# First query projection from features that are scaled by the gain alone, with the token's norm factor applied to its results

## The chip, the cores and the metric

The kernel runs on one core of one Trainium2 chip. The metric is the device time of one execution in microseconds, as the median of several runs. Five engines work side by side: TensorE (PE, with its weight loads as PEld), VectorE (DVE), ScalarE (ACT), GpSimd (POOL) and SyncE (SP), which here issues nearly all DMAs. Each takes its instructions in order, and semaphores tie them together.

## What is computed

The program runs three blocks one after the other over 256 tokens of 1024 features. Only the start of the first block matters here:

```python
def rmsnorm(x, g):
    xf = x.astype(jnp.float32)
    y = xf * lax.rsqrt(jnp.mean(xf * xf, axis=-1, keepdims=True) + EPS)
    return (y * g.astype(jnp.float32)).astype(x.dtype)

h = rmsnorm(x, attn_norm_g)
m = rmsnorm(mem, mem_norm_g)
proj = h @ w_in
da_q, da_k, da_v, wa_q, wa_k, wa_v, xa_q, gates = jnp.split(proj, offsets, axis=-1)
```

Here `da_q` is the first query projection, 1024 columns of `w_in`. After the attention block come a mixture of 16 experts (each with some 25 MB of weights), a second block of two attention layers, and a third block of feed-forward, gating and recurrent layers.

## The kernel before

Activations lie feature-major: 8 blocks of 128 features on the partitions, each with 256 tokens (so a tile of 128x256 is one block, called f or k below). Every dense product is made of three passes in a reduced format: a float32 matrix is split into a high part (rounded, type fp32r) and a low part (the rest), and `t_three` issues high times high (L578), high times low (L579) and low times high (L580).

Weights come from memory in loads of 1 MB, which are numbered: loads 0 to 3 are the four chunks of the first query projection (`daq`), loads 4 to 7 those of the first key projection (`dak`), and so on. They go into four staging slots in turn. ScalarE makes the high part in two halves (`a_hi`, L540, 128x1024 each), then VectorE the low part in two halves (`v_lo`, L551), and both write one of two pairs of buffers, so that load i+2 can be split only as TensorE has read load i, half by half. A chunk of a projection is 48 matrix products of 128x256: half 0 of its weights (blocks k 0 to 3) and then half 1 (k 4 to 7), each for two output tiles. The result of a chunk fills one PSUM bank of 128x512.

The start of the program goes so. ScalarE squares x (L882, four instructions). TensorE sums the squares over the features with a matrix of 1/1024 (L873, `t_rms`), then runs eight products without use on the table `ones` (`t_idle`, L623). ScalarE takes the root (L900, `a_sd`), VectorE the reciprocal (L905, `v_rstd`) into the tile RSTD. Then VectorE makes the normed x block by block (L912: x times gain times RSTD), ScalarE rounds it to the high part (L895, `a_normed`), VectorE subtracts to get the low part (L918), and TensorE starts chunk 0 of `daq` as soon as block 0 is there. All of the nine projections of x read this one pair H.

ScalarE copies each bank of `daq` out with the factor 0.125 (L831). The norm of the second input `mem` follows the same pattern during `dak` and overwrites RSTD. The order on each engine is written out by hand (`t_mix`, `a_mix`, `v_mix`). Projections are generators whose steps are called in turn: one step splits load c+1, the next takes the result of chunk c out. SyncE issues the loads in order and waits, before each, until the two splits of the slot's earlier load have been made.

Of the kernel before, what the change touches and what calls it, by code (L numbers as in the profile page):

```python
# [8 lines left out]
ALU = mybir.AluOpType  # L9
ACT = mybir.ActivationFunctionType  # L10
AX = mybir.AxisListType
P = 128
T = 256
# [148 lines left out]
class Ring:  # L162
# [3 lines left out]
    def next(self):  # L166
        self.i += 1
        return self.ids[(self.i - 1) % len(self.ids)]
# [22 lines left out]
def run(g):  # L191
    for _ in g:
        pass


def F(ap, n=8):
    return ap.rearrange("p (f t) -> p f t", f=n)


def f_(ap):  # L200
    return ap.bitcast(F32)
# [6 lines left out]
def tm(ap):  # L208
    return ap.rearrange("p (t n) -> p t n", t=2)


def both(pair, fn):
    return fn(pair[0]), fn(pair[1])


def it(bank):
    return bank.rearrange("p (i t) -> p i t", t=T)
# [11 lines left out]
class Program:  # L229
# [58 lines left out]
    def B(self, i, n=1):  # L288
        return self.U_(12 + 2 * i, 2 * n)
# [894 lines left out]
    def mix_places(self):  # L1184
        B, R = self.B, self.R
        self.x = B(0)
        self.H = both(self.XP, F)
        self.mp = both(self.pr(6, 7), F)
        self.daq, self.dak, self.dav, self.waq, self.mk, self.mv, self.xaq = B(3), B(4), B(5), B(6), B(9), B(8), B(1)
        self.wak, self.wav = F(B(7)[:, 0:512], 2), tm(B(7)[:, 1024:1536])  # L1190
        self.odt, self.merged = B(2), B(5)
        self.op, self.xp2, self.mgp = self.pr(3, 4), self.pr(6, 2), self.pr(8, 9)
        self.NLAM, self.SUBG = self.LV[:, 5:6], self.LV[:, 6:7]

    def t_mix(self, e):
        DB, KB, OB = Ring(0, 1), Ring(2, 3, 4, 5, 6, 7, 0, 1), Ring(6, 7)
        H, mp, act = self.H, self.mp, self.act
        for w in self.Tw.new(self.first_all):
            e.wait_ge(*w)
        self.t_rms(e, "n1", self.B(9), KB)  # L1200
        self.t_idle(e, 7, 8)
        daq = self.t_proj(e, "daq", 4, H, self.halves("n1"), DB, self.by_act("daq"))
        run(daq)
        dak = self.t_proj(e, "dak", 4, H, self.halves("n1"), KB, self.by_act("dak"))
        next(dak)
        for w in self.Tw.new(self.rest_all):
# [83 lines left out]
    def a_mix(self, e):  # L1290
        act = self.act
        for j in range(4):
            self.a_square(e, "n1", self.x, self.B(9), j, [self.first_all])
        self.a_hi(e, 0, 0)
        self.a_sqrt_table(e)
        self.a_hi(e, 0, 1)
        self.a_sd(e, "n1", 1e-6)
        self.a_next = 1
        self.a_upto(e, 1)
        self.a_normed(e, "n1", self.B(8), self.XP)  # L1300
        daq, dak = self.a_proj(e, "daq", 4, self.a_copy(F(self.daq), 0.125)), self.a_proj(e, "dak", 4, self.a_copy(F(self.dak)))
        for step in range(7):
            next(daq)
        for w in self.Aw.new(self.rest_all, self.dve.val("lam_sums")):
            e.wait_ge(*w)
        e.activation(self.LV[:, 2:4], self.LV[:, 0:2], ACT.Exp).then_inc(*act.inc("lam_exp"))
# [4 lines left out]
        for c in range(4):  # L1311
            next(dak)
            if c == 0:
                self.a_sd(e, "mem", 1e-6)
            next(dak)
            self.a_normed(e, "mem", self.B(8), self.pr(6, 7), range(2 * c, 2 * c + 2))
# [81 lines left out]
    def v_mix(self, e):  # L1398
        dve, LV, LAM = self.dve, self.LV, self.LAM
        for eps, column in self.EPS.items():  # L1400
            e.memset(column, eps).then_inc(*dve.inc(*(["eps"] if eps == 64e-5 else [])))
        for w in self.Vw.new(self.first_all):
            e.wait_ge(*w)
        self.v_upto(e, 0)
        self.v_rstd(e, "n1")
        run(self.v_normed(e, "n1", self.x, self.B(8), lambda f: ("attn_norm_g", f), self.XP))
        daq, dak = self.v_proj(e, "daq", 4), self.v_proj(e, "dak", 4)
        for step in range(5):
            next(daq)
        for w in self.Vw.new(self.rest_all):  # L1410
# [116 lines left out]
        def gained(e, name, c):  # L1527
            residual(e, name, c)
            for f in (2 * c, 2 * c + 1):
                for w in self.Vw.new(dve.val(("out", name, c))):  # L1530
                    e.wait_ge(*w)
                e.tensor_scalar(F(self.h2)[:, f, :], F(self.x)[:, f, :], self.V("ffn_norm_g", f), None, ALU.mult).then_inc(*dve.inc(("ffn", "o", f)))
# [1852 lines left out]
```

## Time and profile before

| | us |
|---|---|
| median of 3 runs | 2803.73 |
| lowest and highest | 2801.77, 2806.78 |
| the profiled execution | 2804.14 |
| its span in the trace | 2802.1 |

| engine | busy, us | share of the span |
|---|---|---|
| PE (matrix products) | 2345.7 | 84% |
| PEld (weight loads) | 1675.2 | 60% |
| DVE | 1227.8 | 44% |
| ACT | 932.8 | 33% |
| POOL | 61.2 | 2% |

All times of the trace are from the start of the span. The profile says busy time per engine; the two stretches to look at are the first 60 us, in which the change lies, and 420 to 1344 us, in which the experts' weights stream in and the DMA engines are full. Where a group of instructions is given with its count, its time runs from the start of the first to the end of the last, and instructions of one engine overlap a little: two of one kind that follow each other start closer together than one lasts.

### The profile page before, as it was taken

The page shows a single profiled execution, that of the slowest core. Times are in us where ns is not written, and L with a number is a line of the kernel's source. Part 1 is how long each engine was busy: PE and PEld are TensorE (multiplying, and loading weights), DVE is VectorE, ACT ScalarE, POOL GpSimd, SP SyncE. Part 2 cuts the span into 40 slices and gives each one's busy share as a digit, 9 for nine tenths or more (in the row PEclk, how much of TensorE's full clock was granted, in tenths as well). Part 3 has the DMA queues.
Part 4 walks back from the last instruction along what each step waited for, and adds up shares of the span by engine and source line. Part 5 has one row for each costly group of instructions (what it writes and reads, how often), then busy time and mean ns, then how long its engine had stood idle before and what let it go on. Part 6 is the DMA issues. An engine that isn't in the chain of part 4 may idle for free.

```text
span 2802.1 us, 37705 instructions
## 1 busy us (share of the span) xinstructions
PE 2345.7 (84%) x16482; PEld 1675.2 (60%) x16482; DVE 1227.8 (44%) x1751; ACT 932.8 (33%) x1524; POOL 61.2 (2%) x36
## 2 busy tenths in 40 slices
PE   8999998656665665566889899999999999977998
PEld 8897784111211121111668778888787888876787
DVE  5567562000100010000476755576656547744654
ACT  5556541000000000000455544354444444632442
POOL 0000010000000000000000000000000000041000
PEclk9999999878888788877989999999999999999999
DMA  7543469999999999999624265575555653412552
GB/s 237 171 157 117 139 209 418 428 428 428 427 428 428 427 428 427 428 428 428 236 76 148 96 198 191 178 241 195 180 181 185 195 206 106 155 34 77 185 191 91
DMA packets 248645, 695.46 MB, mean 248 GB/s; under 512 B 11648, under 2 KB 191104, under 8 KB 222112
## 3 DMA queue, kind: packets, MB, share of 16 engines
q1 hardware_dynamic: 246176, 679.16, 63.7%
q0 software_dynamic: 2016, 13.67, 1.4%
q8 instruction: 130, 2.13, 0.3%
q14 instruction: 35, 0.29, 0.0%
q10 hardware_dynamic: 288, 0.22, 0.0%
HBM read 691.96 MB, written 1.05 MB: 247 GB/s over the span
## 4 chain that ended last, share of the span: by engine, by line
PE 57%; DMA 29%; DVE 8%; ACT 3%; issue 2%; SPq 1%; POOL 0%; DVEq 0%; ACTq 0%
PE ps L578 15%; PE ps L580 15%; PE ps L579 15%; DMA af<-in_w_exp_up 15%; DMA af<-in_w_exp_gate 7%; DMA af<-in_w_exp_down 6%; PE ps L1654 2%; DVE ar L551 2%; PE ps L2594 1%; SPq L509 1%; PE ps L873 1%; PE ps L1684 1%; ACT af L1053 1%; PE ps L2189 1%; DVE af L1089 1%
## 5 line engine op out<-in xcount | busy, mean ns | idle before, releaser
L578 PE MATMUL ps<-ar 128*128 128x512 f32 (+2 forms) x2648 | 928.0, 350 | 27.8 <-DVE ar L551 7.4
L580 PE MATMUL ps<-ar 128*128 128x512 f32 (+2 forms) x2648 | 909.6, 344 | 0.0
L579 PE MATMUL ps<-ar 128*128 128x512 f32 (+2 forms) x2648 | 909.6, 343 | 0.0
L551 DVE TENSOR_TENSOR ar<-af,ar 128x1024 fp32r<-128x1024 f32 x516 | 604.3, 1221 | 290.3 <-ACT ar L540 290.2
L578 PEld LDWEIGHTS ps<-ar 128*128 128x128 f32 x2648 | 504.2, 190 | 104.9 <-issue 11.6
L540 ACT ACTIVATE ar<-af 128x1024 fp32r<-128x1024 f32 x516 | 511.3, 1047 | 164.5 <-PE ps L580 149.1
L580 PEld LDWEIGHTS ps<-ar 128*128 128x128 f32 x2648 | 504.5, 191 | 59.2
L579 PEld LDWEIGHTS ps<-ar 128*128 128x128 f32 x2648 | 505.0, 191 | 56.2 <-issue 0.5
L1654 PE MATMUL ps<-af 128*32 128x512 f32 x2048 | 325.5, 769 | 233.3 <-DMA af<-in_w_exp_up 126.8
L1654 PEld LDWEIGHTS ps<-af 128*32 128x32 f32 x2048 | 63.6, 126 | 480.1 <-DMA af<-in_w_exp_up 199.5
L1823 DVE TENSOR_TENSOR af<-af,ps 128x512 f32<-128x512 f32 x16 | 11.0, 687 | 541.0 <-ACT af L1730 541.0
L1684 PE MATMUL ps<-af 128*32 128x512 f32 x1024 | 168.9, 790 | 93.8 <-DMA af<-in_w_exp_down 82.4
L1730 ACT ACTIVATE af<-ps 128x512 f32<-128x512 f32 x16 | 9.6, 597 | 593.6 <-PE ps L1654 593.6
L1541 DVE TENSOR_TENSOR af<-ps,af 128x512 f32<-128x512 f32 x76 | 48.5, 684 | 299.6 <-PE ps L1696 270.3
L1684 PEld LDWEIGHTS ps<-af 128*32 128x32 f32 x1024 | 35.2, 129 | 210.2 <-DMA af<-in_w_exp_down 140.3
L1737 ACT ACTIVATE af<-ps 128x512 f32<-128x512 f32 x16 | 9.6, 597 | 269.1 <-PE ps L1684 269.1
L2249 DVE TENSOR_TENSOR af<-af,ps 128x256 f32<-128x256 f32 x66 | 27.8, 421 | 125.0 <-ACT af L2220 124.9
L2220 ACT ACTIVATE af<-ps 128x256 f32<-128x256 f32 x66 | 25.3, 384 | 135.7 <-PE ps L580 135.7
L1053 ACT ACTIVATE af<-af,sm 128x256 f32<-128x256 f32 (+1 forms) x136 | 64.0, 474 | 17.1 <-DVE sm L1136 10.2
L2594 PE MATMUL ps<-af 64*64 64x64 f32 x2304 | 44.3, 229 | 20.8 <-issue 16.7
L2594 PEld LDWEIGHTS ps<-af 64*64 64x64 f32 x2304 | 41.2, 141 | 24.5 <-issue 20.0
L2211 ACT ACTIVATE ar<-ps 128x512 fp32r<-128x512 f32 x44 | 26.3, 598 | 81.6 <-PE ps L2189 81.6
(313 smaller groups left out, 1634.8 us busy)
## 6 DMA issues: line engine op xcount, KB each, us to landing
af<-in_w_exp_gate SPq DMA_DIRECT2D x64, 2048.0 KB, 41.2
af<-in_w_exp_up SPq DMA_DIRECT2D x64, 2048.0 KB, 40.8
af<-in_w_exp_down SPq DMA_DIRECT2D x63, 2048.0 KB, 41.5
af<-in_ffn_w_in SPq DMA_DIRECT2D x88, 1024.0 KB, 5.8
af<-in_ffn_w_out SPq DMA_DIRECT2D x44, 1024.0 KB, 5.1
af<-in_w_in SPq DMA_DIRECT2D x34, 1024.0 KB, 5.2
af<-in_sgu_w_in SPq DMA_DIRECT2D x16, 1024.0 KB, 7.0
af<-in_w_out SPq DMA_DIRECT2D x12, 1024.0 KB, 5.3
```

What stands on the lines that cost most here:

```text
L509: e.dma_start(view(base), src).then_inc(*(self.row_in[r] if q == self.tail else self.landed[load.slot]).one())
L540: e.activation(self.WH[load.pair][:, c], self.base(i)[:, c], ACT.Copy).then_inc(*self.act.inc(("hi", i, h)))
L551: e.tensor_tensor(self.WL[load.pair][:, c], self.base(i)[:, c], f_(self.WH[load.pair][:, c]), ALU.subtract).then_inc(*self.dve.inc(("lo", ...
L578: e.matmul(o, lh, rh, start=start, stop=False, skip_group_check=True)
L579: e.matmul(o, lh, rl, start=False, stop=False, skip_group_check=True)
L580: return e.matmul(o, ll, rh, start=False, stop=stop, skip_group_check=True)
L873: m = e.matmul(self.bank(name)[:, 0:T], self.C("ones"), F(tmp)[:, f, :], start=first and n == 0, stop=last and n == len(fs) - 1, skip_grou ...
L1053: e.activation(d, d, ACT.Exp, bias=st[:, g:g + 1], accum_out=st[:, 4 + g:5 + g]).then_inc(*self.act.inc((name, "e", i, g)))
L1541: e.tensor_tensor(d, it(self.bank((name, c))), d, ALU.add).then_inc(*self.dve.inc(("out", name, c)))
L1654: t = e.matmul(ps[32 * j:32 * j + 32, bb, :], XE[:, k, c:c + 32], k_(self.base(q), 2)[:, r, 512 * j:512 * j + 512], start=k == 0, stop=k == 7)
L1684: t = e.matmul(ps[o:o + 32, b, :], self.AT_[x % 2][:, r * P + 32 * j:r * P + 32 * j + 32], k_(self.base(q), 4)[:, r, 512 * c:512 * c + 512 ...
L2594: t = e.matmul(self.ps[64 * r:64 * r + 64, banks[n], 64 * c:64 * c + 64], left(tt, h, i, cp), right(tt, h, i, cp), start=True, stop=True)
```

## The change

A new pair of tiles, `xg`, holds x times the gain (`attn_norm_g`), high and low part, without the token's factor. It lies in room that is free until the norm of `mem` needs part of it. ScalarE makes the high parts (`gained`, a Copy with a scale per partition) and VectorE the low parts (`gained_lo`), in turn with the two halves of load 0. `daq` multiplies `xg`, and needs neither root nor reciprocal. Each chunk's result is then taken out by VectorE instead of ScalarE, in `q_out`: times 0.125 and times RSTD. The eight products without use are gone. The pair H is still made, for the other projections, but later: VectorE makes its parts behind `q_out` of chunks 0 to 2, and ScalarE behind the splits of loads 2, 3 and 4. One wait is added: ScalarE takes the root for `mem`, which overwrites RSTD, only when VectorE has taken out chunk 3.

```diff
+        self.xg = both(self.pr(5, 6), F)
...
-        self.t_idle(e, 7, 8)
-        daq = self.t_proj(e, "daq", 4, H, self.halves("n1"), DB, self.by_act("daq"))
-        run(daq)
+        run(self.t_proj(e, "daq", 4, self.xg, self.halves("xg"), DB, self.by_dve("daq")))
...
+        gained = lambda j: self.a_gained_hi(e, "xg", self.x, self.xg[0], lambda f: self.V("attn_norm_g", f), j, [])
+        gained(0)
         self.a_hi(e, 0, 0)
+        gained(1)
+        self.a_hi(e, 0, 1)
+        gained(2)
+        gained(3)
         self.a_sqrt_table(e)
-        self.a_hi(e, 0, 1)
         self.a_sd(e, "n1", 1e-6)
         self.a_next = 1
         self.a_upto(e, 1)
-        self.a_normed(e, "n1", self.B(8), self.XP)
-        daq, dak = self.a_proj(e, "daq", 4, self.a_copy(F(self.daq), 0.125)), self.a_proj(e, "dak", 4, self.a_copy(F(self.dak)))
+        daq, dak = self.a_proj(e, "daq", 4), self.a_proj(e, "dak", 4, self.a_copy(F(self.dak)))
         for step in range(7):
             next(daq)
+            if step in (2, 4, 6):
+                self.a_normed(e, "n1", self.B(8), self.XP, {2: (0, 1, 2), 4: (3, 4, 5), 6: (6, 7)}[step])
...
             if c == 0:
+                for w in self.Aw.new(self.dve.val(("out", "daq", 3))):
+                    e.wait_ge(*w)
                 self.a_sd(e, "mem", 1e-6)
...
-        self.v_upto(e, 0)
+        def gained_lo(j):
+            for f in (2 * j, 2 * j + 1):
+                for w in self.Vw.new(self.act.val(("xg", "h", f))):
+                    e.wait_ge(*w)
+                e.scalar_tensor_tensor(out=self.xg[1][:, f, :], in0=F(self.x)[:, f, :], scalar=self.V("attn_norm_g", f), in1=f_(self.xg[0][:, f, :]),
+                                       op0=ALU.mult, op1=ALU.subtract).then_inc(*dve.inc(("xg", "l", f)))
+        gained_lo(0)
+        self.v_lo(e, 0, 0)
+        gained_lo(1)
+        self.v_lo(e, 0, 1)
+        self.v_next = 1
+        gained_lo(2)
+        gained_lo(3)
         self.v_rstd(e, "n1")
-        run(self.v_normed(e, "n1", self.x, self.B(8), lambda f: ("attn_norm_g", f), self.XP))
-        daq, dak = self.v_proj(e, "daq", 4), self.v_proj(e, "dak", 4)
+        n1 = self.v_normed(e, "n1", self.x, self.B(8), lambda f: ("attn_norm_g", f), self.XP)
+
+        def q_out(e, name, c):
+            for w in self.Vw.new(self.pe.val(("ps", name, c)), dve.val(("n1", "rstd"))):
+                e.wait_ge(*w)
+            e.scalar_tensor_tensor(out=F(self.daq)[:, 2 * c:2 * c + 2, :], in0=it(self.bank((name, c))), scalar=0.125,
+                                   in1=self.RSTD.unsqueeze(1).broadcast_to((P, 2, T)), op0=ALU.mult, op1=ALU.mult).then_inc(*dve.inc(("out", name, c)))
+            for step in range(4 if c < 2 else 2 if c == 2 else 0):
+                next(n1, None)
+        daq, dak = self.v_proj(e, "daq", 4, q_out), self.v_proj(e, "dak", 4)
```

The first instructions of VectorE before, from the two halves of load 0 (`sm` holds RSTD, `ar` the split pairs, `vec` the gains):

```order
L551 TENSOR_TENSOR ar<-af,ar 128x1024 x2
L905 RECIPROCAL sm<-sm 128x256
L912 SCALAR_TENSOR_TENSOR af<-af,vec,sm 128x256 x3
L918 TENSOR_TENSOR ar<-af,ar 128x256
L912 SCALAR_TENSOR_TENSOR af<-af,vec,sm 128x256
```

The same place on VectorE now, up to the first halves of load 2 (L1415 is `gained_lo`, L1430 is `q_out`):

```order
L1415 SCALAR_TENSOR_TENSOR ar<-af,vec,ar 128x256 x2
L551 TENSOR_TENSOR ar<-af,ar 128x1024
L1415 SCALAR_TENSOR_TENSOR ar<-af,vec,ar 128x256 x2
L551 TENSOR_TENSOR ar<-af,ar 128x1024
L1415 SCALAR_TENSOR_TENSOR ar<-af,vec,ar 128x256 x4
L905 RECIPROCAL sm<-sm 128x256
L551 TENSOR_TENSOR ar<-af,ar 128x1024 x2
L1430 SCALAR_TENSOR_TENSOR af<-ps,sm 128x512
L912 SCALAR_TENSOR_TENSOR af<-af,vec,sm 128x256 x3
L918 TENSOR_TENSOR ar<-af,ar 128x256
L912 SCALAR_TENSOR_TENSOR af<-af,vec,sm 128x256
L918 TENSOR_TENSOR ar<-af,ar 128x256
```

The halves of load 1 stand ahead of the normed blocks now, and directly behind the reciprocal.

ScalarE before, from the squares to the first result taken out:

```order
L882 ACTIVATE af<-af 128x512 x4
L540 ACTIVATE ar<-af 128x1024
L753 ACT_TABLE_LOAD
L753 ACTIVATE sm<-sm 128x1
L540 ACTIVATE ar<-af 128x1024
L900 ACTIVATE sm<-ps,sm 128x256
L540 ACTIVATE ar<-af 128x1024 x2
L895 ACTIVATE ar<-af 128x256 x8
L831 ACTIVATE af<-ps 128x512
```

ScalarE now, over the same part (L1876 is `gained`):

```order
L882 ACTIVATE af<-af 128x512 x4
L1876 ACTIVATE ar<-af,vec 128x256 x2
L540 ACTIVATE ar<-af 128x1024
L1876 ACTIVATE ar<-af,vec 128x256 x2
L540 ACTIVATE ar<-af 128x1024
L1876 ACTIVATE ar<-af,vec 128x256 x4
L753 ACT_TABLE_LOAD
L753 ACTIVATE sm<-sm 128x1
L900 ACTIVATE sm<-ps,sm 128x256
L540 ACTIVATE ar<-af 128x1024 x4
L895 ACTIVATE ar<-af 128x256 x3
L540 ACTIVATE ar<-af 128x1024 x2
```

The root (L900) and the halves of load 1 (the first two of the L540 x4) have moved behind eight gained blocks and the table load; the rounding of the normed blocks (L895) has moved behind the splits of loads 2, 3 and 4.

## Rows read from the trace of the kernel before

**Rows 1.** Busy time by stretch: us, PE, PEld, DVE, ACT, POOL; PEclk, DMA share, GB/s.

```profile
0.00:60.00 60.00, 50.86 (x362) 48.28 (x363) 30.02 (x51) 33.96 (x51) 0.20 (x4) 1.00 0.76 251
60.00:150.00 90.00, 90.00 (x569) 79.38 (x569) 54.98 (x71) 48.57 (x86) 0.00 (x0) 1.00 0.51 167
...
410.00:420.00 10.00, 10.00 (x86) 10.00 (x85) 7.63 (x12) 4.84 (x7) 0.00 (x0) 1.00 0.26 76
420.00:1344.00 924.00, 576.43 (x3626) 167.94 (x3625) 83.32 (x160) 28.49 (x50) 0.00 (x0) 0.82 1.01 427
```

**Rows 2.** TensorE in order of time: start, duration, line, tiles, count, idle before.

```profile
7.74 5.60 PE L873 MATMUL ps<-af,cst 128*128 128x256 f32 x16 [7.74 <-ACT af L882]
13.17 3.62 PE L623 MATMUL ps<-cst 128*128 128x256 f32 x16
17.76 0.35 PE L578 MATMUL ps<-ar 128*128 128x256 f32 x1 [0.97 <-ACT ar L895]
...
18.50 0.35 PE L578 MATMUL ps<-ar 128*128 128x256 f32 x1
...
24.70 0.28 PE L578 MATMUL ps<-ar 128*128 128x256 f32 x1
```

**Rows 3.** ScalarE in order of time, same columns.

```profile
6.96 2.19 ACT L882 ACTIVATE af<-af 128x512 f32<-128x512 f32 x4 [3.95 <-DMA cst<-in_consts]
9.53 1.06 ACT L540 ACTIVATE ar<-af 128x1024 fp32r<-128x1024 f32 x1 [0.38 <-DMA af<-in_w_in]
10.61 1.28 ACT L753 ACT_TABLE_LOAD   x1
11.90 0.20 ACT L753 ACTIVATE sm<-sm 128x1 f32<-128x1 f32 x1
12.01 1.04 ACT L540 ACTIVATE ar<-af 128x1024 fp32r<-128x1024 f32 x1
13.37 0.47 ACT L900 ACTIVATE sm<-ps,sm 128x256 f32<-128x256 f32 x1 [0.32 <-PE ps L873]
13.74 1.99 ACT L540 ACTIVATE ar<-af 128x1024 fp32r<-128x1024 f32 x2
...
31.15 2.00 ACT L540 ACTIVATE ar<-af 128x1024 fp32r<-128x1024 f32 x2
36.91 2.00 ACT L540 ACTIVATE ar<-af 128x1024 fp32r<-128x1024 f32 x2
```

**Rows 4.** VectorE in order of time, same columns.

```profile
13.08 1.22 DVE L551 TENSOR_TENSOR ar<-af,ar 128x1024 fp32r<-128x1024 f32 x1 [1.13 <-ACT ar L540]
14.23 1.74 DVE L905 RECIPROCAL sm<-sm 128x256 f32<-128x256 f32 x1
16.00 1.28 DVE L912 SCALAR_TENSOR_TENSOR af<-af,vec,sm 128x256 f32<-128x256 f32 x3
17.20 0.42 DVE L918 TENSOR_TENSOR ar<-af,ar 128x256 fp32r<-128x256 f32 x1
17.53 0.48 DVE L912 SCALAR_TENSOR_TENSOR af<-af,vec,sm 128x256 f32<-128x256 f32 x1
```

**Rows 5.** Instructions elsewhere in the program of the kinds that the change adds.

```profile
1358.35 0.91 ACT L1849 ACTIVATE ar<-af,sm 128x256 fp32r<-128x256 f32 x2 [0.33 <-DVE af L1541]
...
1358.89 0.88 DVE L1857 SCALAR_TENSOR_TENSOR ar<-af,sm,ar 128x256 fp32r<-128x256 f32 x2
...
L1481 DVE SCALAR_TENSOR_TENSOR af<-af,ps x12: 678/686/689, 268.3 to 399.3; 128x512 f32<-128x512 f32 x12
```

**Rows 6.** SyncE's queue: issues in order, then size and us to landing of four windows.

```profile
7.22 3.03 SPq L509 DMA_DIRECT2D af<-in_w_in  x1
...
17.46 0.43 SPq L517 DMA_DIRECT2D cst<-in_consts  x1
...
af<-in_w_in SPq DMA_DIRECT2D x1, 1024.0 KB, 13.8
...
cst<-in_consts SPq DMA_DIRECT2D x1, 1240.0 KB, 11.3
...
af<-in_w_in SPq DMA_DIRECT2D x1, 1024.0 KB, 13.6
```

The windows of rows 6 begin at 9.6 us (the issue at 7.22, load 3), at 17.4 us (the late constants) and at 18.0 us (load 4, issued at 18.01).

## What the change should do to the time

> **What bounds the kernel now.** I read the stretches first [rows 1]. From 60 to 150 us TensorE is busy for all of the 90 us, and up to 60 us for 50.86; from 420 to 1344 us the DMA engines are full (share 1.01 at 427 GB/s) while TensorE works 576 of 924 us. So the program is bound by TensorE at first and by the experts' weights later. The change lies in the first 40 us; the question is when TensorE gets its first work, and whether time won there lasts to the end.
>
> The second view is TensorE's own order of time [rows 2]. It sums the squares from 7.74 us, is through at about 13.2, then does 3.62 us of products without use, and starts the first real product at 17.76. The next starts of L578 show the second loss: 18.50 is 0.74 after 17.76, with three products between. Chunk 1 starts at 24.70. Later chunks are 5.76 us apart, as ScalarE's splits show, which follow TensorE's release of the buffers (31.15 and 36.91) [rows 3]; that is 0.36 for three of a chunk's 48 products. So chunk 0 took 6.94 us instead of 5.76 and began 4.6 us after the sums.
>
> The third view says why [rows 3, 4]: the root ends at 13.84, the reciprocal at 15.97, the first normed block is split by 17.6, and then VectorE needs 0.73 us a block (16.00 and later: 17.20 to 17.93 is one pair). That chain is what the change takes out of the way.
>
> **What the change removes.** At best chunk 0 starts at the end of the sums, at the place where the filler began, 13.17, and runs without gaps: 13.17 + 5.76 = 18.93, against 24.70. That is the upper bound of the gain, 5.77 us: 4.59 of earlier start, 1.18 of the stretch.
>
> **Can the operands be there?** The costs come from relatives of the new instructions [rows 5]: two gained blocks on ScalarE take 0.91 us together, so they start 0.40 apart and last 0.50; two gained low parts on VectorE 0.88, so 0.40 apart and 0.48 long.
> ScalarE: squares are through at 9.15, the next may start at 9.06. Gained 0 and 1 at 9.06 and 9.46, half 0 of load 0 from 9.86 to 10.90 (1.04 long, 0.95 apart [rows 3]; load 0 lands at 9.53), gained 2 and 3 at 10.8 and 11.2, half 1 from 11.6 to 12.65, gained 4 to 7 from 12.55 to 14.26. Then the table load, 1.28, and the small root, next start 1.40 after the load's (10.61 to 12.01 before): root at 15.67 to 16.14, halves of load 1 at 16.04 to 17.1 and 17.0 to 18.0.
> VectorE: gained low 0 and 1 by 10.6; low half 0 of load 0 from 11.04 to 12.26; gained low 2 and 3 by 13.06; low half 1 from 12.98 to 14.2 (1.15 apart [rows 4]); gained low 4 to 7 by 15.8. Then the reciprocal, 16.27 to 18.01, and low halves of load 1 at 17.95 to 19.17 and 19.1 to 20.3.
> TensorE needs blocks 0 to 3 and low half 0 in the first 2.88 us and has them all by 13.06; blocks 4 to 7 and low half 1 by 16.05 and has them by 15.8. So chunk 0 runs from 13.17 to 18.93. Chunk 1 needs low half 0 of load 1, made at 19.17: with 0.11 us for the signal it starts at 19.28. The reciprocal stands in front of it and costs 0.35. The gain so far: 24.70 - 19.28 = **5.42 us**.
>
> **Does TensorE stay fed after that?** VectorE now has more per chunk: a result taken out, 0.69 [rows 5], four steps of the norm at up to 0.73, 2.9 [rows 4], and a split, 2.36; in all 5.9 beside a chunk of 5.76. It is nearly the bound, so I followed it through. Result 0 from 20.2 (result ready at about 19.2), three normed blocks and two low parts by 23.1, low halves of load 2 by 24.3 and 25.5; chunk 2 is due at 25.04. Result 1 from 25.4, four blocks and four low parts by 29.0, load 3 by 30.2 and 31.3; chunk 3 is due at 30.80. Four small instructions for lambda (they wait for the late constants, 17.46 + 11.3 = 28.8 [rows 6]), result 2, the last two low parts, load 4 half 0. Of these the low parts wait for ScalarE, which rounds blocks 6 and 7 behind both halves of load 4, and load 4 lands at 18.01 + 13.6 = 31.6 [rows 6]. Halves 31.7 to 33.6, blocks by 34.3, last low part by 34.85, low half 0 of load 4 by 36.0. The first key chunk is due at 19.28 + 3 x 5.76 = 36.56. So each chunk is met, with 0.4 to 0.7 us to spare; there lies the risk. Loads 2 and 3 are no risk: load 3 lands at 7.22 + 13.8 = 21.0 and is split after 23.
>
> ScalarE loses four results to take out (some 0.6 each) and gains eight blocks of 0.4: its work moves, and none of it is awaited. The added wait, root of `mem` behind result 3, comes in the middle of the first key chunk plus its sums: result 3 is out at about 37.8, the sums of `mem` end near 43. It costs nothing; what queues behind it on ScalarE, the copy of that chunk's result, is no earlier than the sums either. SyncE's order is unchanged; the slot of load 1 frees four us sooner (20.3 against 24.2), which only moves a load behind others in the same queue.
>
> **Does it last?** Between 60 and 420 us every slot and buffer is released by TensorE or what follows it, and all of that moves with it. The experts' stream is a fixed 924 us, but its start is not fixed: in the ten us before it the DMA share is 0.26 [rows 1], so it starts when places come free, that is, with the work before it. Behind it all is released by its end. I carry 5.42 through in full.
>
> The sum: profiled execution 2804.14 - 5.42 = 2798.7; that execution lies 0.4 above the median, so against the median 2803.73 - 5.42 = **2798.3 us**.
>
> **The clock, where a rule speaks against the change.** The sums of squares took 5.60 us for 16 passes, the filler 3.62 for as many [rows 2], though the granted clock in the rows is 1.00 [rows 1]: by the spacing, TensorE started at its lower level (1.2 GHz) and had reached 2.4 before the filler. In the trace, about 1 us idle between filler and first product did not bring it back: the products that follow run at the high rate. Now there is no filler, and one gap of 0.35 us. If the level fell all the same and came back as at the start, it would cost about 5.60 - 3.62 = 2.0 us: 2800.3. The Trainium skill, "TensorE: Matmul & The Clock Gate", section "HAM oscillation — how this bites in real kernels", says that waits between bursts of products make the array fall back to its lower clock; by that rule the filler was worth keeping, while the trace has a longer wait without a fall.
>
> **The table load.** It stood in the shadow of load 0's second half and now stands ahead of the root, so all its time counts. Here it lasts 1.28, starts 0.02 after the instruction before it and lets the next start at once [rows 3]. If it cost twice that, root, reciprocal and load 1 would come 1.3 later, chunk 1 at 20.6: gain 4.1, 2799.6. The Trainium skill, "ScalarE: Activation LUTs", section "What ACT_TABLE_LOAD costs", gives 1.28 us and a drain of 1.38 on top; the rows show no such drain.
>
> **The rivals.**
> Something in the chain of VectorE and ScalarE between 20 and 37 us comes late by more than its 0.4 to 0.7 us of room: each us more is lost once. With 1 to 3 us the gain is 2.4 to 4.4, time 2799.3 to 2801.3. Against it: all durations are measured ones. For it: four margins in a row.
> The gain is swallowed by the expert stream, if its first loads are held by something other than the work before. Gain 0, 2803.7. Against it the share of 0.26.
> Slower: load 4 is late. Blocks 6 and 7 of the pair H, without which no key chunk starts, are now behind its landing on ScalarE. Before, it landed at 31.6 and was due at 41.97, with 8 us of room behind it; now the room is 0.5, and past 32.1 every us of delay costs one. Slower than before from a landing at 37.5, slower by the 5.6 us that count from 43. It is issued and served behind the late constants, in a queue that the change does not lengthen, and the landings in the rows are 11 to 14 us after issue, so this is unlikely.
> The change doesn't do what it says: chunk 0 still waits, because eight gained blocks on ScalarE hold up load 0. By the working above they do so by 0.4 us where it isn't needed yet.
>
> **How the numbers follow.** Forecast, gain 5.0 to 5.8: 0.72. Late chain or table or clock, 2 to 4.5: 0.17. Swallowed: 0.07. Slower: 0.04. A measurement tells about 0.2% from no change, 5.6 us here; the forecast of 5.4 lies just below. Of its 0.72 I give 0.36 to a measured gain above 5.6 and 0.36 below, and the next two cases wholly to "within": faster 0.36, same 0.60, slower 0.04. The range: 2803.7 - 5.8 = 2797.9, less the 2 us by which the lowest run lay under the median, 2795.9; upward it takes in the late chain, 2801.3, and the same 2 us: 2803.3.
>
> **What would show it.** Right: the first L578 at 13.2, chunk 1 at 19.3, the first key chunk at 36.6, 5.4 us less in every later stretch's start, the expert stream starting that much earlier. Wrong: TensorE waiting for L551 or L918 after chunk 1 (chain late), for L873's spacing to return in L578 to L580 (clock), an expert stream that starts where it did.

## The result, and the profile after

| | us |
|---|---|
| before, median of 5 runs | 2802.41 (2801.71 to 2806.78) |
| the changed kernel, median of 5 runs | 2789.04 (2787.60 to 2790.55) |
| ratio | 0.995, 95% interval 0.9938 to 0.9961 |
| span of the profiled execution | 2788.1, against 2802.1 |

The kernel became 13.4 us faster. The forecast was 5.4 us faster and a range down to 2795.9, so the direction was right and the size was not.

The place of the change looks as forecast. TensorE in the changed kernel, in order of time (start, duration, line, tiles, count, idle before):

```profile
7.88 5.25 PE L873 MATMUL ps<-af,cst 128*128 128x256 f32 x16 [7.88 <-ACT af L882]
12.78 0.47 PE L578 MATMUL ps<-ar 128*128 128x256 f32 x1
13.09 0.28 PE L579 MATMUL ps<-ar 128*128 128x256 f32 x1
...
19.18 0.38 PE L578 MATMUL ps<-ar 128*128 128x256 f32 x1 [0.31 <-DVE ar L551]
...
36.56 0.28 PE L578 MATMUL ps<-ar 128*128 128x256 f32 x1
```

These rows answer to [rows 2]: the first product comes right behind the sums, chunk 1 at 19.18 (24.70 before) after the small wait for load 1's low half, and the first key chunk, whose start was 41.98 before, at 36.56. VectorE and ScalarE in the same stretch (L1876 is `gained`):

```profile
16.30 1.75 DVE L905 RECIPROCAL sm<-sm 128x256 f32<-128x256 f32 x1 [0.42 <-ACT sm L900]
17.97 2.29 DVE L551 TENSOR_TENSOR ar<-af,ar 128x1024 fp32r<-128x1024 f32 x2
...
35.03 2.35 DVE L551 TENSOR_TENSOR ar<-af,ar 128x1024 fp32r<-128x1024 f32 x2
```

```profile
12.69 1.70 ACT L1876 ACTIVATE ar<-af,vec 128x256 fp32r<-128x256 f32 x4
14.40 1.28 ACT L753 ACT_TABLE_LOAD   x1
...
15.81 0.46 ACT L900 ACTIVATE sm<-ps,sm 128x256 f32<-128x256 f32 x1
...
32.01 2.01 ACT L540 ACTIVATE ar<-af 128x1024 fp32r<-128x1024 f32 x2 [4.45 <-DMA af<-in_w_in]
```

So where are the other 8 us? I took the same instruction in both traces, the low split (L551, 516 of them, numbered from 0), as a mark of time, and asked by how much the changed kernel was ahead of the one before, stretch by stretch:

| stretch | before, us | after, us | won in it |
|---|---|---|---|
| start of the program to split 12 | 53.64 | 48.22 | 5.42 |
| to split 108 (end of the attention block) | 339.17 | 339.52 | -0.35 |
| to split 120 (the experts) | 976.69 | 977.88 | -1.19 |
| to split 438 (second block, most of the third) | 1059.00 | 1059.01 | 0.0 |
| to split 450 (the chunked scan of the third block) | 169.99 | 159.83 | **10.16** |
| to split 515, the last | 178.21 | 178.22 | 0.0 |

The scan is code that the change doesn't touch. Most of its products are small: 2304 of 64x64 in one line (L2594 before, L2621 after) and some 1200 others. Here is its stretch in both kernels, busy time first (us, PE, PEld, DVE, ACT, POOL; PEclk, DMA share, GB/s), then the group of the small products (busy, mean ns, idle before it and what ended it), then, for before, the DMA queue that carries instructions (packets, MB, share). Before:

```profile
2428.50:2598.50 170.00, 133.60 (x3537) 117.54 (x3536) 84.06 (x111) 54.55 (x93) 40.68 (x12) 0.95 0.19 60
...
L2594 PE MATMUL ps<-af 64*64 64x64 f32 x2304 | 44.3, 229 | 20.8 <-issue 16.7 <-DVE af L3156 3.7 <-ACT af L2956 0.4
...
q8 instruction: 28, 0.46, 1.1%
```

After:

```profile
2424.60:2584.40 159.80, 131.52 (x3537) 115.30 (x3537) 84.41 (x110) 54.40 (x93) 40.71 (x12) 0.97 0.20 65
...
L2621 PE MATMUL ps<-af 64*64 64x64 f32 x2304 | 44.7, 228 | 17.1 <-issue 15.5 <-DVE af L3183 1.6
```

Same products, the same 28 packets of instructions in both, but less idle time "issue", that is, time in which TensorE waits for nothing that the profile shows. In the chain of waits of this stretch "issue" has 16.8% of 170.0 us before, 28.6 us, and 14.1% of 159.8 after, 22.5 us. A close look at one such pause of before, from the chain of waits (start, us, what):

```profile
2532.96 1.82 issue
...
2535.10 1.92 PE ps L2594 x123
2537.02 3.97 issue
2540.99 3.94 PE ps L2594 x129
```

The row of the stretch behind the long pause, with the same columns as above:

```profile
2540.90:2544.20 3.30, 3.21 (x118) 3.22 (x122) 1.29 (x2) 1.00 (x2) 0.00 (x0) 0.50 0.02 5
```

Between the two pauses TensorE does about 128 products, with as many weight loads, 256 instructions. The packets of the queue are 0.46 MB / 28 = 16 KB, so 64 bytes for each of 256 instructions. In the trace's packet records one begins at 2531.87, the next at 2538.61, within the long pause and lasting 1.04; in the scan none follows another by less than 3.2 us in any trace here, while TensorE, once it has instructions, needs 1.92 us for 123 products with their weight loads.

The instruction records say it more sharply. Number all of TensorE's records (products, weight loads and semaphore instructions) from 0 at the start of the program. In the scans of the 14 traces of this case there are 163 pauses of over 0.8 us at whose end no semaphore is waited for, and every one of them stands ahead of the same place of a piece: a number that leaves 193 when divided by 256. I take that place for the begin of a piece. All 163 end 0.5 to 1.6 us behind the end of the latest packet, 1.4 in the median. In the scan TensorE waits for its own program. The Trainium skill, "Advanced Engine Details and Errata", section "ISA Cache", gives a cache line of 16 KB, 256 instructions; the packets agree.

The row after the long pause shows a second cost: 129 products took 3.94 us, where 123 took 1.92 before it. That is the lower of the clock's two levels: the granted clock is 0.50 in those 3.3 us, after a pause of 3.97 us. Over the whole stretch it is 0.95 before and 0.97 after.

The filler that the change deletes is 16 products and 16 weight loads in the trace, 32 instructions, an eighth of a piece. So everything behind it moves in the pieces, and pieces begin at other places of the scan. That is the theory to be tested: **the length of TensorE's program ahead of the scan decides how long the scan takes**. Its rivals: the new instructions on VectorE and ScalarE, which lengthen those programs; the earlier start; a difference between single executions; and that fewer instructions are faster wherever they stand.

### The profile page after: what moved, and what is told of

It is laid out like the page before. It is cut to its first block, busy times and chain, and to the rows that moved or that the text cites. A ratio compares the mean times of both kernels' runs of the same rounds, so it can differ in the third digit from the quotient of the medians.

```text
span 2788.1 us, 37692 instructions
## 1 busy us (share of the span) xinstructions
PE 2338.4 (84%) x16466; PEld 1670.5 (60%) x16466; DVE 1233.6 (44%) x1763; ACT 933.2 (33%) x1528; POOL 61.3 (2%) x36
## 4 chain that ended last, share of the span: by engine, by line
PE 57%; DMA 29%; DVE 8%; ACT 3%; issue 1%; SPq 1%; POOL 0%; ACTq 0%; DVEq 0%
PE ps L578 16%; PE ps L580 15%; PE ps L579 15%; DMA af<-in_w_exp_up 13%; DMA af<-in_w_exp_down 8%; DMA af<-in_w_exp_gate 7%; PE ps L1681 2%; DVE ar L551 2%; PE ps L2621 1%; SPq L509 1%; PE ps L1711 1%; PE ps L873 1%; ACT af L1053 1%; PE ps L2216 1%; DVE af L1089 1%
## 5 line engine op out<-in xcount | busy, mean ns | idle before, releaser
L551 DVE TENSOR_TENSOR ar<-af,ar 128x1024 fp32r<-128x1024 f32 x516 | 604.7, 1221 | 269.6 <-ACT ar L540 269.5
L540 ACT ACTIVATE ar<-af 128x1024 fp32r<-128x1024 f32 x516 | 511.4, 1047 | 169.2 <-PE ps L580 150.9
L1053 ACT ACTIVATE af<-af,sm 128x256 f32<-128x256 f32 (+1 forms) x136 | 64.0, 474 | 17.2 <-DVE sm L1136 10.2
L2621 PE MATMUL ps<-af 64*64 64x64 f32 x2304 | 44.7, 228 | 17.1 <-issue 15.5
L2621 PEld LDWEIGHTS ps<-af 64*64 64x64 f32 x2304 | 41.4, 139 | 20.9 <-issue 18.6
```

The source lines that it names most:

```text
L540: e.activation(self.WH[load.pair][:, c], self.base(i)[:, c], ACT.Copy).then_inc(*self.act.inc(("hi", i, h)))
L551: e.tensor_tensor(self.WL[load.pair][:, c], self.base(i)[:, c], f_(self.WH[load.pair][:, c]), ALU.subtract).then_inc(*self.dve.inc(("lo", ...
L1053: e.activation(d, d, ACT.Exp, bias=st[:, g:g + 1], accum_out=st[:, 4 + g:5 + g]).then_inc(*self.act.inc((name, "e", i, g)))
L2621: t = e.matmul(self.ps[64 * r:64 * r + 64, banks[n], 64 * c:64 * c + 64], left(tt, h, i, cp), right(tt, h, i, cp), start=True, stop=True)
```

## The experiments

Two kinds of edits serve most of them. One removes the filler of the kernel before. The other adds n short useless products of 128x32 ahead of expert 8, in the stretch in which TensorE is idle over a third of the time [rows 1]. A short product is two products and two weight loads in the trace, four instructions. The runs were made in three groups, each beside the kernel before on the same chip, and the ratios are against it: its medians were 2801.25, 2803.18 and 2801.13.

```python
    def t_short(self, e, b, n):
        free = self.take(b, "idle")
        for i in range(n):
            for w in self.Tw.new(*free):
                e.wait_ge(*w)
            e.matmul(self.ps[:, b, 0:32], self.C("ones"), self.cst[:, 0:32], start=True, stop=True)
```

**Without the filler, nothing else changed.**

```diff
-        self.t_idle(e, 7, 8)
```

> The kernel before without the eight products without use behind the sums of squares (8 of 128x256, which the trace shows as 16 products and 16 weight loads, 32 instructions of TensorE); nothing else is changed, the output is the same. Fetch theory (the 10 us that the change won beyond its own place come in the third block's chunked scan, because TensorE's program got 32 instructions shorter ahead of it and so the 16 KB pieces in which it is fetched begin at other places of the scan): the first real product stays at 17.8 us, everything up to 2380 us stays within 0.5 us, the scan from 2440 to 2580 us is 10 us shorter, in all about 2792. Rival (the scan's gain came from the earlier start, from the new instructions of VectorE and ScalarE, or from luck of the run): 2802, no change.

Measured: 2796.91 (2793.97 to 2799.36, 10 runs), ratio 0.9985 (0.9976 to 0.9994). The scan takes 163.1 us instead of 170.0. But the start did not stay as it was: the first product comes at 18.00 (17.76 before), chunk 1 at 25.78 (24.70 before). TensorE's first product, and the row of the stretch behind it:

```profile
18.00 0.36 PE L578 MATMUL ps<-ar 128*128 128x256 f32 x1 [4.42 <-ACT ar L895]
...
18.70:22.10 3.40, 3.37 (x15) 3.37 (x16) 3.40 (x11) 1.68 (x4) 0.00 (x0) 0.50 0.78 229
```

Without the filler TensorE is idle for 4.42 us, and from 18.7 to about 22.1 the products start 0.21 apart instead of 0.12, at a granted clock of 0.50. So the filler did keep something: chunk 0 takes 7.78 us without it and 6.94 in each of the five traces of this start with it. In the second trace without it (`b_nofill_other` below) TensorE is idle for 4.99 us, the granted clock is 0.50 from 17.4 to 24.1, and chunk 0 takes 8.78.

Removing eight products 2400 us ahead shortens the scan by 7 us and lengthens the start by 1. In all 4.3 us are won: more than the rival's zero, less than I expected.

**The changed kernel, made as long as before again.**

```diff
         for x in range(16):
+            if x == 8:
+                self.t_short(e, TB.ids[TB.i % 4], 8)
             ba, bu = EB.next(), EB.next()
```

> The changed kernel with eight short products without use (8 of 128x32) put ahead of expert 8, where TensorE has some 35% of idle time; they make TensorE's program as long as before again for all that follows. Fetch theory: chunk 1 of the first query projection still starts at 19.2, the second block still starts 3.9 us earlier than before, but the scan takes as long as before again; in all 2798 to 2799. Rival: 2789, as the changed kernel, since the products lie beside the loads.

Measured: 2792.87 (2788.5 to 2796.72, 10 runs), ratio 0.9971 (0.9961 to 0.998); scan 164.2 us. The start is nearly as in the changed kernel (split 12 at 48.57). It is slower than the changed kernel by 4 us (its ratio was 0.9938 to 0.9961), in the direction of the theory but by half of what it said.

**A whole piece, and half a piece.**

> As the last, with 64 short products: 128 products and 128 weight loads in the trace, 256 instructions, which at 64 bytes each is one whole fetched piece of 16 KB. Fetch theory: the pieces begin at the same places of the scan as in the changed kernel, so the scan takes as long as there: 2789. If instead any added instruction costs the 10 us: 2799. Rival (no influence of the program's length): 2789 as well.

> As the last, with 32 short products, half a piece. Fetch theory: the pieces begin half a piece elsewhere; the scan's length changes by some us, either way, 2784 to 2802, and differs from the changed kernel's 2789 by more than 1. Rival: 2789.

Measured: with 64, 2790.29 (2787.47 to 2791.76, 4 runs), ratio 0.996 (0.9945 to 0.9975), scan 160.9 us, as the changed kernel. With 32, 2784.27 (2783.97 to 2787.76, 4 runs), ratio 0.9943 (0.9928 to 0.9957), scan 155.8 us: it has 128 instructions more than the changed kernel and a lower median. With 8 and with 32 the ratios are clear of each other (0.9961 to 0.998 against 0.9928 to 0.9957), and no rival explains that 32 are faster than 8. The difference of 64 from 8, and of 32 from the changed kernel, lies within the intervals.

**The same two kernels once more.**

> The changed kernel, unchanged, beside the next ones on one chip. Fetch theory: about 2789 to 2790; the scan stretch (428.5 us before the end of the feed-forward loads' order, that is from the 439th to the 451st low split of the list, 159.8 us in the first profile) within 2 us of that. If the scan's length was luck of single runs, the median lies near 2796 (2801 less the 5 us of the start).

> The kernel before, unchanged, for one more profile: how far does the scan's time differ between two executions of one program? Fetch theory: within 2 to 3 us of the 170.0 of the first profile. Luck: anywhere from 156 to 170, the spread of the programs so far.

Measured: the changed kernel 2787.36 (2786.43 to 2789.63, 4 runs), ratio 0.9948 (0.9933 to 0.9963); its scan 156.5 us, against 159.8 in the first profile, so more than the 2 us that I allowed it. The kernel before: one execution, 2802.74, scan 167.5, against 170.0. A scan of one program differs by about 3 us between two executions. The two programs are further apart than that, by 7.7 us at the least and 13.5 at the most.

**The kernel before with nothing but useless work added.**

```diff
         for x in range(16):
+            if x == 8:
+                self.t_short(e, TB.ids[TB.i % 4], 24)
             ba, bu = EB.next(), EB.next()
```

> The kernel before with nothing changed at its start and 24 short products without use (128x32) ahead of expert 8. With its own 8 of the start it has as many TensorE instructions ahead of the scan as the changed kernel with 32 short products, whose scan took 155.8 us. Fetch theory: the same scan, 156 +- 2 us, so the whole 12 to 14 us below the kernel before: 2788, by nothing but added useless work. Rival: 2801, no change.

Measured: 2791.21 (2790.25 to 2796.02, 5 runs), ratio 0.9963 (0.9949 to 0.9977); scan 156.5 us. This is the sharpest of the runs: the start is untouched (chunk 0 takes 6.94 us), 48 products and 48 weight loads are added, and the program is 12 us faster. In the scan the small products now wait less:

```profile
2429.10:2585.60 156.50, 132.72 (x3538) 116.19 (x3537) 85.18 (x111) 54.45 (x93) 40.70 (x12) 0.96 0.20 65
...
L2604 PE MATMUL ps<-af 64*64 64x64 f32 x2304 | 44.4, 227 | 14.6 <-issue 12.6 <-DVE af L3166 1.7 <-ACT af L2966 0.4
```

PE busy 132.7 us against 133.6, idle for "issue" in this group 12.6 against 16.7; in the chain of waits 11.0% of 156.5, 17.2 us, against 28.6. The 11.4 us less of "issue" are nearly the whole 13.5 by which the scan is shorter.

**A quarter of a piece.**

> The changed kernel with 16 short products (64 instructions, a quarter of a piece) ahead of expert 8. Fetch theory: a scan between the ones with 8 (164.2 us) and with 32 (155.8 us), about 160; in all 2785 to 2792. Rival: as the changed kernel beside it.

Measured: 2790.98 (2789.29 to 2792.23, 4 runs), ratio 0.9959 (0.9944 to 0.9974), scan 163.0 us. The time lay in the range, the scan 3 us above what I expected. From this one scan, with 3 us between executions, nothing follows on how it falls between 8 and 32.

**The kernel before with a whole piece in all.**

> The kernel before with 56 short products ahead of expert 8. With its own 8 these are 64, 256 instructions, so the pieces of TensorE's program begin in the scan where they do in the kernel without the filler. Fetch theory: scan 160 to 163 us, in all about 2796, below the kernel before although 224 instructions are added. Rival (shorter is faster, whatever the place): 2802 or more.

Measured: 2794.52 (2791.23 to 2795.98, 9 runs), ratio 0.9976 (0.9966 to 0.9986), scan 159.7 us, near the kernel without filler. 224 added instructions make it faster by 6.6 us, so "a shorter program is faster" is out; the place is what counts. Here the filler is kept, so chunk 0 takes 6.94 us, and this run shows what the place alone is worth between these two settings.

**The programs of VectorE and ScalarE.** The change also adds 12 instructions to VectorE and 4 to ScalarE.

```diff
+        for again in range(12):
+            e.memset(self.SM2[:, 200 + again:201 + again], 0.0).then_inc(*dve.inc())
         e.tensor_tensor(self.G20, gf, gn, ALU.mult).then_inc(*dve.inc("g20"))
...
+            if x == 8:
+                for again in range(4):
+                    e.activation(self.SM2[:, 220 + again:221 + again], self.G20[:, 0:1], ACT.Copy).then_inc(*act.inc())
```

> The kernel before, filler kept, with the same 12 memsets and 4 copies. If VectorE's or ScalarE's program length matters by itself: scan 164 us instead of 167 to 170, in all about 2798. If only TensorE's matters: 168 us, 2802.

> The kernel before without the eight products of the start, and with 12 one-column memsets on VectorE and 4 one-column copies on ScalarE in the expert stage, where both engines idle: the programs of all three engines are then as long, ahead of the scan, as in the changed kernel, while the start is that of before. If the lengths of all three programs matter: scan 156 to 160 us as in the changed kernel, in all 2792 to 2794. If only TensorE's matters: scan 163 us as without the filler alone, 2797.

Measured: with the filler, 2801.27 (2797.05 to 2806.06, 10 runs), ratio 0.9999 (0.999 to 1.0009), scan 170.0 us: the lengths of the two other programs do nothing by themselves. Without it, 2795.03 (2791.45 to 2799.95, 10 runs), ratio 0.998 (0.9971 to 0.999), scan 160.4. That scan is what the rival of this run expected, but it lies within 3 us of the 163.1 without the additions, and the two medians (2796.91, 2795.03) lie nearer than their runs spread.

**The best version of both.**

```diff
         gained_lo(3)
+        self.v_lo(e, 1, 0)
         self.v_rstd(e, "n1")
+        self.v_lo(e, 1, 1)
+        self.v_next = 2
...
+            if x == 8:
+                self.t_short(e, TB.ids[TB.i % 4], 32)
```

> The changed kernel with two edits: low half 0 of load 1 is made ahead of the reciprocal, not behind it, so that chunk 1 does not wait (it should start at 18.9 instead of 19.2; gain 0.3 us); and 32 short products ahead of expert 8, the number with the shortest scan so far (155.8 us). Both theories of the start: 0.3 us. In all 2783.5 to 2785, about 17 us below the kernel before.

Measured: 2786.28 (2783.74 to 2787.57, 4 runs), ratio 0.9946 (0.9931 to 0.996), scan 156.8 us. The median lies 1.3 us above what I expected. In its trace the sums end late, the first product comes at 13.48, and chunk 1 begins at 19.41 with no idle time ahead of it:

```profile
19.41 0.28 PE L578 MATMUL ps<-ar 128*128 128x256 f32 x1
```

But in three traces of the changed start without that edit chunk 1 begins without a wait too (a_short16, a_short32, a_short64: the first product at 13.19 to 14.06, chunk 1 5.9 us later). Whether there is a wait to be saved depends on when the sums end, and against the same kernel without that edit (2784.27) nothing is won.

**All scans, by where the pieces begin.** The first column counts useless products ahead of the scan, modulo a piece (64).

| useless products | kernels with the start of before: scan us, total | with the changed start: scan us, total |
|---|---|---|
| 8 | 170.0, 167.5, 170.0; 2801.1 to 2803.2 | 164.2; 2792.9 |
| 0 or 64 | 163.1, 160.4, 159.7; 2796.9, 2795.0, 2794.5 | 159.8, 156.5, 160.9; 2789.0, 2787.4, 2790.3 |
| 16 | | 163.0; 2791.0 |
| 32 | 156.5; 2791.2 | 155.8, 156.8; 2784.3, 2786.3 |

Down a column the place of the pieces changes the total by 7 to 12 us; neighbouring rows are not all clear of each other. Along a row the start changes it by 4 to 10. The traces place the start's part better, since the scan's spread is not in it. The first key chunk starts at 41.98 to 42.84 in the five traces of the start of before with its filler (mean 42.46), and at 36.56 to 38.08 in the seven of the changed start (mean 37.11): 5.4 us. At split 438, ahead of the scan, the means are 2429.3 and 2423.9, again 5.4 us. In the row of 8 the scans still differ by 3 to 6 us for the same place of the pieces; that is not explained.

## Why the prediction was wrong, point by point

**What bounds the start: right, with some luck in the number.** The first product came at 12.78 for a forecast of 13.17, chunk 1 at 19.18 for 19.28. The term 5.42 measured 5.42 at the first key chunk and at split 12 in the first pair of traces, and 5.4 in the means; the single traces of one start lie up to 1.5 us apart there, so the second decimal is chance.

**Operands in time: right.** Four gained blocks on ScalarE took 1.70 us (forecast by [rows 5] 1.71), the reciprocal began at 16.30 (16.27), low half 0 of load 1 at 17.97 (17.95), `q_out` took 0.68 (0.69). The one wait ahead of chunk 1 was idle time of 0.31, for 0.35; against steady products it cost 0.46, because chunk 0 was through 0.4 us earlier than forecast. The 0.11 us for the signal has no row behind it, and the trace shows less: the first of the two halves that start at 17.97 is done at 19.13, and the product starts at 19.18.

**TensorE stays fed: right in the first trace, and the rival of load 4 did come, in small.** The last low part of the pair H waited for ScalarE behind load 4, which landed near 32 (the row at 32.01), and low half 0 of load 4 began at 35.03 and ended at 36.2; TensorE came to it at 36.56. So the room was 0.3 us and not 0.5. In other executions with the same start load 4 lands later. In `a_short64`:

```profile
33.78 2.01 ACT L540 ACTIVATE ar<-af 128x1024 fp32r<-128x1024 f32 x2 [5.76 <-DMA af<-in_w_in]
...
38.08 0.39 PE L578 MATMUL ps<-ar 128*128 128x256 f32 x1 [0.84 <-DVE ar L551]
```

In the seven traces of this start ScalarE begins load 4 between 31.86 and 33.78, and in three of them TensorE is idle for 0.23, 0.66 and 0.84 us ahead of the first key chunk. The rival called this unlikely; it has the right place and costs at most 1 us here. Before, with 8 us of room, it couldn't cost anything.

**The clock: no loss in the changed kernel, but for a reason that the prediction didn't give.** From the second product on the starts are 0.12 apart: right behind the sums there is no idle time in which the level could fall. The rule of the Trainium skill ("TensorE: Matmul & The Clock Gate", "HAM oscillation — how this bites in real kernels") does show in two places. Where only the filler was removed, TensorE was idle for 4.42 us and ran at a granted clock of 0.50 behind it; so in the kernel before the filler was worth 0.8 to 1.8 us of chunk 0. In the scan it is the pause of 3.97 us, with half the rate behind it. The change could delete the filler only because it also removed the wait that the filler bridged.

**The table load: 1.28, no more.** It began 0.01 after the gained blocks ended and the root came 1.41 after its start. The drain that the Trainium skill adds ("ScalarE: Activation LUTs", section "What ACT_TABLE_LOAD costs") is not in this trace either.

**Does it last: right up to the scan.** The lead was 5.07 us at the end of the attention block and 3.9 behind the experts. The 1.2 us lost there were that execution's: over all traces that stretch takes 976.7 to 978.3 us, with either start.

**The step that failed** stands in two sentences of the prediction: "That is the upper bound of the gain, 5.77 us", where the filler's deletion counts only by its place in time, and "Behind it all is released by its end", by which everything later is a pure shift. Deleting 32 TensorE instructions also shifts the rest of the program in its fetched pieces, a term put at nothing without a reason. By the medians it was worth 4 to 7 us (4.3 and 6.1 with the filler deleted, 6.6 where instructions were added to reach the same place), in a stretch that I never looked at. The two profiles differ there by 10.2 us; of that some 8 are the place (169.2 us in the mean of three traces with it, 161.1 of three without), and the rest is no more than the spread of one scan. The forecast got its direction from the start, which was right; that the larger part of the gain had the same sign was luck, for the prediction had no term for it. The profile before shows the place: behind the experts TensorE's longest wait in total is "issue" ahead of L2594, 16.7 us in ten pauses, the longest 3.97. Had I read those, a change of program length would have been a term with both signs and some 7 us of size, and the range would have had to hold it.

## What to carry to other kernels

Where a stretch issues small TensorE instructions faster than they are fetched, as the scan does here, its time depends on how many instructions stand ahead of it, by as much as a whole optimisation elsewhere. So a change that adds or removes instructions has to be compared stretch by stretch, and by kernels that are padded to the same place in the pieces, before its gain is credited to its idea. And padding is a tool of its own: here 24 useless products in an idle stretch gave the unchanged kernel 12 us. Before a filler is deleted, ask what it bridges: with the wait still there, its deletion cost 0.8 to 1.8 us at its own place.

## What the runs showed of the hardware

TensorE's instructions come in packets of 16 KB, 256 instructions. In the scan the packets' starts were never under 3.2 us apart and in the median 3.8 to 4.2, while TensorE ran through 123 products and their weight loads in 1.92 us. Over the 14 scans a packet starts 1.2 us (median) after TensorE has passed into the piece before it, lasts about 1.1, and TensorE goes on 1.4 behind its end. These three add up to an estimate of 3.7 us for a piece, near the distance of the starts. So in the scan a piece is fetched only once the one before it is begun.

The start of the packet is later while weight loads run. Where the loads kept the 16 DMA engines over half busy between TensorE's passing and the packet (54 cases), it was 2.6 us in the median; where they took under 2% (303 cases), 1.15. All pauses of over 2.5 us followed a packet that began 2.6 to 3.8 us late, with the loads taking 0.6 to 0.99 of the engines. The four best scans, 155.8 to 156.8 us, have at most one pause between 2.5 and 3.5 us; the three of 167.5 to 170.0 us have one or two of 2.9 to 4.0.

Pauses of over 0.8 us at a piece's begin add up to 25.1 us (14 of them) in the first profile of the kernel before, and to 11.8 (9) in the kernel before with 24 short products. A part of the spread of one kernel's runs, some 5 us, comes from here: the scan of one program differed by up to 3.4 us between two executions, while the stretch ahead of it (split 420 to split 438, 95.9 us) agreed within 0.02 in all traces. The rest of the spread is not placed. What decides which places are good (whether a piece begins on a wait for another engine, or while a load runs) was not tried by itself; it is argued from the pauses, while the dependence on the place is shown.
